# A transformer of four layers on one core: who sums a norm's squares, and where the last column is added

## The reference

```
y = x * rsqrt(mean(x*x, over the 1024 features) + 1e-6) * g
h = y * (1 + scale) + shift
x = x + gate * sublayer(h)
```

## Time and profile before

| | us |
|---|---|
| median of three timed runs | 2603.38 (2601.52 to 2606.22) |
| profiled execution, its own time | 2600.84 |
| its span in the trace | 2599.0 |
| TensorE busy | 2448.9 (94%) |
| VectorE busy | 1545.6 (59%) |
| ScalarE busy | 964.5 (37%) |
| mean granted clock of TensorE | 0.972 of 2.4 GHz |

### The profile page before, as it was taken

One profiled execution on the slowest core, in us unless ns is written; L12 is line 12 of the kernel. 1 busy time (PEld: TensorE's weight loads), 2 busy tenths in 40 slices (PEclk: granted clock), 3 DMA queues, 4 the chain that ended last, 5 costly groups with the idle time before them and its releaser, 6 DMA issues.

```text
span 2599.0 us, 33645 instructions
## 1 busy us (share of the span) xinstructions
PE 2448.9 (94%) x13706; PEld 1960.6 (75%) x13706; DVE 1545.6 (59%) x2408; ACT 964.5 (37%) x1751; POOL 201.6 (8%) x157
## 2 busy tenths in 40 slices
PE   5998899999999999989999889999989999989997
PEld 3875565678888888878876767887778867868775
DVE  4256667548767666665426588878762346363454
ACT  4355567533122121234234332322353135353352
POOL 1000001001101011110001011201100000000010
PEclk8999999999999999999999999999989979999999
DMA  6232100023333433212120244444322110112301
GB/s 238 90 126 87 39 1 1 17 81 114 122 122 106 135 107 102 96 57 73 57 81 1 78 140 163 154 163 156 120 65 65 58 69 1 49 41 81 118 1 65
DMA packets 67002, 223.62 MB, mean 86 GB/s; under 512 B 7328, under 2 KB 11040, under 8 KB 66208
## 3 DMA queue, kind: packets, MB, share of 16 engines
q1 hardware_dynamic: 63504, 211.51, 24.3%
q10 hardware_dynamic: 3344, 9.96, 1.0%
HBM read 219.34 MB, written 2.10 MB: 85 GB/s over the span
## 4 chain that ended last, share of the span: by engine, by line
PE 83%; DVE 9%; ACT 4%; DMA 3%; issue 1%; SPq 0%; ACTq 0%; DVEq 0%
PE pair L1098 21%; PE pair L1099 20%; PE pair L1100 20%; PE pair L1277 5%; PE side L1328 4%; DMA RAW<-in_w 3%; PE pair L1315 3%; DVE T L1987 2%; DVE ACC L1976 1%; PE side L1315 1%; DVE WL L1833 1%; PE pair L1124 1%; ACT WH L1427 1%; PE pair L774 1%; DVE HL L1995 1%
## 5 line engine op out<-in xcount | busy, mean ns | idle before, releaser
L1098 PE MATMUL pair<-HH,WH 128*128 128x512 f32 (+1 forms) x2496 | 881.1, 353 | 37.3 <-DVE HL L1995 28.1
L1099 PE MATMUL pair<-HL,WH 128*128 128x512 f32 (+1 forms) x2496 | 870.7, 349 | 0.0
L1100 PE MATMUL pair<-HH,WL 128*128 128x512 f32 (+1 forms) x2496 | 869.7, 348 | 0.0
L1427 ACT CAST WH<-RAW 128x1024 fp32r<-128x1024 f32 (+4 forms) x286 | 271.4, 949 | 877.8 <-DMA RAW<-in_w 874.7
L1833 DVE TENSOR_TENSOR WL<-RAW,WH 128x1024 fp32r<-128x1024 f32 (+4 forms) x286 | 314.2, 1099 | 470.1 <-ACT WH L1427 458.9
L1098 PEld LDWEIGHTS pair<-HH,WH 128*128 128x128 f32 x2496 | 477.4, 191 | 113.7 <-DVE HL L1995 34.1
L1100 PEld LDWEIGHTS pair<-HH,WL 128*128 128x128 f32 x2496 | 477.2, 191 | 59.9
L1099 PEld LDWEIGHTS pair<-HL,WH 128*128 128x128 f32 x2496 | 477.6, 191 | 59.2 <-issue 1.2
L1976 DVE SCALAR_TENSOR_TENSOR ACC<-MODW,CVF,ACC 128x512 f32<-128x512 f32 x364 | 324.9, 951 | 0.0
L1098 PE MATMUL pair<-DH,WH 128*128 128x512 f32 (+1 forms) x624 | 226.9, 364 | 4.5 <-DVE X L1902 3.6
L1099 PE MATMUL pair<-DL,WH 128*128 128x512 f32 (+1 forms) x624 | 220.0, 353 | 0.0
(11 more groups left out here) (318 smaller groups left out, 2576.9 us busy)
## 6 DMA issues: line engine op xcount, KB each, us to landing
RAW<-in_w SPq DMA_DIRECT2D x242, 512.0 KB, 3.5
MODW<-in_w SPq DMA_DIRECT2D x104, 512.0 KB, 4.4
RAW<-in_w SPq DMA_DIRECT2D x48, 384.0 KB, 3.1
RAW<-in_w SPq DMA_DIRECT2D x16, 256.0 KB, 2.6
DFL<-in_dft_lat ACTq DMA_DIRECT2D x4, 1024.0 KB, 7.7
X<-in_x ACTq DMA_DIRECT2D x8, 384.0 KB, 10.6
out_x<-X SPq DMA_DIRECT2D x8, 256.0 KB, 2.0
RAW<-in_w SPq DMA_DIRECT2D x8, 192.0 KB, 2.3
```

Of the source, the lines that this page charges most:

```text
L1098: mm(out[0:j.m, c:e], wh[k], a, start=k == 0, stop=False)
L1099: mm(out[0:j.m, c:e], wh[k], b, start=False, stop=False)
L1100: ins = mm(out[0:j.m, c:e], wl[k], a, start=False, stop=k == j.k - 1)
L1427: nc.scalar.copy(WH[:, j.n % NRING, 0:c], RAW[:, j.n % NRING, 0:c]).then_inc(*act.mark("hi", j.n))
```

## The change

It has two parts. In five norms (all but s1) VectorE's running sum ends with feature 4; TensorE takes four terms for each token part, the square of feature 5, the running sum of features 0 to 4, and the squares of features 6 and 7, each with a wait of its own. The last square gets a buffer of its own (T[3]) and no longer waits for a running sum. And in the four phases whose columns end in a norm, VectorE adds the last column to X first and makes the low half of the weight three jobs ahead behind it, at the end of the phase.

```
@@ norm_sums, TensorE's program
             take(2)
-            pe.wait_ge(*step("nacc", q["id"], KD - 2))
             for s, a, b in lat_first(q["t0"]):
-                pe.wait_ge(*step("nsq", q["id"], s, KD - 1))
-                sums_of(s, T[2][:, a:b], T[1][:, a:b], ("nss", q["id"], s))
+                terms = ((("nsq", q["id"], KD - 3), T[1]), (("nacc", q["id"], KD - 4), T[2]),
+                         (("nsq", q["id"], KD - 2), T[0]), (("nsq", q["id"], s, KD - 1), T[3]))
+                for n, (made, t) in enumerate(terms):
+                    pe.wait_ge(*step(*made))
+                    ins = mm(sum_psum(s), ONES, t[:, a:b], start=n == 0, stop=n == 3)
+                ins.then_inc(*pe.mark("nss", q["id"], s))
@@ square, ScalarE's program
-            if k >= 3:
+            if 3 <= k < KD - 1:
                 act.wait_ge(*step("nacc", q["id"], k - 2))
...
-                A(T[1][:, a:b], X[:, k, q["t0"] + a:q["t0"] + b], AF.Square).then_inc(*act.mark("nsq", q["id"], s, k))
+                A(T[3][:, a:b], X[:, k, q["t0"] + a:q["t0"] + b], AF.Square).then_inc(*act.mark("nsq", q["id"], s, k))
@@ accumulate, VectorE's program
-            if k == KD - 1:
+            if k > KD - 4:
                 return
@@ VectorE's program, a phase of jobs
                 js = p[1]
+                nxt = phases[pi + 1] if pi + 1 < len(phases) else None
+                columns = [j for j in js if j.kind == "addx"]
+                last_column = columns[-1] if columns and nxt and nxt[0] == "norm" else None
...
-                        if j.n not in LATE_SPLITS[:-1]:
+                        if j.n not in LATE_SPLITS[:-1] and j is not last_column:
                             split()
...
-                nxt = phases[pi + 1] if pi + 1 < len(phases) else None
                 if nxt and nxt[0] == "norm":
                     dve.also("xready", nxt[1]["id"])
+                if last_column:
+                    split()
```

## The result

The changed kernel took 2580.48 us (median of four runs, 2578.34 to 2584.68), the kernel before 2604.8 on the same chip (four runs, 2601.52 to 2606.84): a ratio of 0.991, interval 0.9891 to 0.9929. Forecast were 2591.2 and a range from 2586 to 2599. So it is faster, by twice the 12.2 us of the sum. With later runs of the same kernel, 16 in all, its median is 2583.7 (2578.34 to 2590.45); 80 runs of the kernel before give 2601.8. 18.1 us is the better figure for the change: of the 6.2 us between it and the first 24.3, 3.2 come from the changed kernel's first four runs, which lie in the lower part of the 16, and 3.0 from the four of the kernel before, which lie above its 80.

The account below looks back on a forecast made before the run. TensorE was taken as the bound, busy 2448.9 of 2599.0 us, so only its standstills pay. Gains at a2, b1, b2 and s0, less hand-over and a1, sum to -12.2 us: 2591.2 from the 2603.38 median, range 2586 to 2599.

Parts of the forecast that it names:

- Last product to logarithm, 3.7 us: Norms a2, b1, b2, s0: four warm terms put the logarithm about 3.7 us after the last product.
- the cold rival: Norms' sums: all four terms run at 1.2 GHz, 7.1 us to the logarithm; +9.1 us, 2612.5; chance 5%.
- the terms were early: Rival for a2, b1, b2, s0: all four terms follow the last square; only -5.0 us, 2598.4; chance 5%.
- products colder: Products behind the norms' sums stay at the low clock 3 us longer, giving back 5.4 us: 2596.6; chance 15%.
- Low half hidden: VectorE after the last column: the moved low half ends before the root, costing at most 1.23 us otherwise in b1.
- a1, +2.3: Norm a1: added terms lie on the chain to the first layer's first weight, costing 2.0 to 2.6, taken as 2.3 us.
- Sum of the norms, -12.2: All five norms: -4.95 (b1), -2.15 (a2), -2.75 (b2), -5.15 (s0), +0.5 hand-over, +2.3 (a1).
- How the numbers follow: Step on chances and range: forecast 65%, own spread 2587 to 2595, range 2586 to 2599, faster beyond 0.2% at 0.87.
- The first reading: Opening step on what bounds the kernel: TensorE's standstills before the norms' sums, 16.0 us together, then its clock.

Follow-up runs that it names:

- e3: Changed kernel without its second part, so the low half stays ahead of the last column: 2589.04 us, ratio 0.995 to the kernel before.
- e13: Kernel before plus spare fp32 matmuls in layer s0's windowed attention, six at its start and one in each pair from 1 to 11: 2600.82 us, ratio 0.9993.
- e14: Changed kernel plus spare fp32 matmuls in layer s0's windowed attention, six at its start and one in each pair from 1 to 11: 2585.03 us, ratio 0.9935.
- e10: Kernel before plus two spare fp32 matmuls inside layer s0's products, some 90 us ahead of the windowed attention: 2598.17 us, ratio 0.9992.
- e9: Kernel before plus one spare fp32 matmul inside layer s0's products, some 90 us ahead of the windowed attention: 2603.37 us, ratio 1.0008.
- e12: Changed kernel with a1's sum as before (full running sum on VectorE, two terms on TensorE), no spare matmuls: 2584.98 us, ratio 0.9943.
- e1: Changed kernel run once more, unedited: 2587.92 us, ratio 0.9941 to the kernel before.
- e11: Kernel before plus three spare fp32 matmuls inside layer s0's products, some 90 us ahead of the windowed attention: 2602.54 us, ratio 1.001.

## Why the prediction was wrong

**Last product to logarithm, 3.7 us: right.** 3.68 in three norms and 4.08 in s0, for 3.73. The clock was 1.00 in these four, so the cold rival is refuted for them, and the terms were early, so that rival is too. The Trainium skill (TensorE: Matmul & The Clock Gate, "A second HAM failure mode: psum-queue depth-cycling") would have had the clock swing at the small waits; no trace of the four-term sums shows it falling in them, in e3 not even with waits of 0.56 us (b1) and 0.65 us (s0) inside. The rival "products colder" didn't come either: behind the sums of a2, b1, b2 and s0 the clock was low for 3.4, 3.4, 6.8 and 3.4 us, where it had been for 3.4, 3.4, 6.8 and 6.8.

**Low half hidden: right.** In b1 it ended 1.0 us ahead of the logarithm.

**a1, +2.3: right at the first weight**, +1.7 to +2.9 in six traces. At the end of the kernel its price is unclear: with a1's sum as before the median moved by -4.1, -0.85 and +1.3 us in three comparisons.

**Sum of the norms, -12.2: right in the mean, in part by luck.** -8.3, -11.3 and -13.3 ahead of layer s0's attention in the changed kernel's three traces, -10.5 between e13 and e14. In the changed kernel's three, the four norms gave 1.0 to 1.3 us more than their terms, and the way to a2 cost 4.1 in the mean for 2.3; the two errors offset each other.

**What failed is the term that isn't in the sum.** TensorE's clock away from the norms was put at nothing, without a reason. The step is "How the numbers follow": "Its own spread is 2587 to 2595: a1 between 2.0 and 5.2 and the clock after the sums." The rival "products colder" also looked for the clock's price right behind the norms only, and only for a loss. It was a gain, and 200 us further on. The first reading already said that the clock was "the second thing to read", but read it around the sums alone. The low spell of layer s0's attention, 37.6 us long in the kernel before, is worth 0.4 us per microsecond (7.0 us for 17.1 less in the changed kernel, 7.2 for 17.1 less in e10, 5.5 for 13.7 less in e9). It was 37.6 us in both traces of the kernel before and 20.5, 34.1 and 13.7 in those of the changed kernel, worth 7.0, 2.0 and 9.7 us. The mean of that, 6.2, with 11.0 for the norms and some 0.6 behind, makes up the 17.8 of the traces. In e12, where the spell was 37.5 us, the trace gained 12.1 us in all, no more than its norms' part of 12.5. A term "clock in the attention, 0 to -10" would have moved the range's low end from 2586 to 2576.

The range also allowed nothing for the scatter of the runs; the three that were known lay within 4.7 us (2601.52 to 2606.22). The changed kernel scatters over 12 us, and its first four runs fell in the lower half of that: this part of the miss is chance.

*What stays open.* Whether the change makes the spell shorter, and by what. The kernel before seems nearly always to have a long one: both of its traces do, and of 95 later runs none was under 2594 us, where one with a spell of 14 us should be near 2592 (an estimate from 2601.8 and 0.4 us per microsecond); three at 2594.2 to 2594.3, with a mean clock of 0.975, fit one of about 20. The changed kernel often has a short one. That the attention starts some 12 us earlier doesn't decide it, as e12 did so too and had 37.5. Nor does the moment at which the clock falls: 0.6 and 0.7 us behind the attention's first product it stayed low for 34.1 (e1) and 20.5 us (the first trace), 3.2 to 3.3 us behind for 37.5 (e12), 30.7 (e3) and 10.2 (e11). What TensorE does there was not varied either: in the kernel before's spell none of its matmuls is a full 128 x 128 one with more than 128 columns, and the spare work of e13 and e14 both added such matmuls and filled idle time. And with the spell out of both, medians give 15.8 us where the norms' part in the traces is 8.3 to 13.3: some 4 us are not placed.

## What to carry to other kernels

List every stretch in which the clock reads low before summing up a change, not only those beside the edit: the length of a spell far from the edit can differ from run to run and from kernel to kernel, and it belongs in the range, with either sign. A wait for a chain of additions can be exchanged for matmuls that TensorE has idle time for anyway; in a2, b1, b2 and s0 the terms started where the last product ended and ran at a clock of 1.00, so the warm price was the right one there. For less than 1%, take more than four runs of each kernel, and find the gain in several traces, place by place, before believing a median.

## What the runs showed of the hardware

The low clock lasted although TensorE was fully busy. In the kernel before it stayed at 0.50 (1.2 GHz) for 14.00 busy of 14 us, and for 37.6 us in all, in the attention's own matmuls; spare fp32 matmuls of 128 x 128 by 512 among them (e13, e14) kept it at 1.00, with TensorE recorded busy for 13.27 to 13.72 of 14 us. So the recorded busy share doesn't tell the clock. Nearly all of the time in that spell went into scores with weights of 64 x 128 (52 records, 12.7 us), transposes (40, 15.4 us), products with weights of 128 x 64 (28, 7.7 us) and matmuls of 2 columns (18, 5.8 us). Whether that has to do with the clock is not shown. The groups, from 2099.6 to 2137.1 us:

```profile
L1277 PE MATMUL pair<-SK,SQT 64*128 64x256 f32 (+1 forms) x52 | 12.7, 620 | 0.0
L1315 PE MATMUL pair<-CONST,T 128*128 128x128 f32 x26 | 9.7, 444 | 0.0
L1328 PE MATMUL side<-PTW,SV 128*64 128x256 f32 x28 | 7.7, 646 | 0.0
L1289 PE MATMUL pair<-SINKR,BAND 128*128 128x2 f32 x18 | 5.8, 354 | 2.4 <-ACT T L1729 2.1
L1315 PE MATMUL side<-CONST,T 128*128 128x128 f32 x14 | 5.7, 438 | 0.0
```

The Trainium skill (TensorE: Matmul & The Clock Gate, "Part 1") has the clock return soon once TensorE is busy; here it didn't, and the measurement decides.

The same program on the same data had spells of 13.7, 20.5 and 34.1 us at this place in three profiled executions, worth 7.7 us between the longest and the shortest; its times scatter over 12.1 us.

A clock of 1.00 in the column doesn't make every group equally fast. At the start of the changed kernel's first trace it reads 1.00 throughout, and yet the same group of eight matmuls took 1.08 us at 25.43 and 0.64 us at 34.71. What slowed the first isn't shown; the DMA engines' share was 0.93 around it and 0.25 around the second:

```profile
25.43 1.08 PE L1072 MATMUL side<-RAW,CVP 128*32 128x256 f32 x8 [0.72 <-ACT AR L1450]
...
34.71 0.64 PE L1072 MATMUL side<-RAW,CVP 128*32 128x256 f32 x8
```
